# Five small moves in a TensorE-bound two-block transformer kernel: piece sizes, load order, and where adds, transposes and copies stand

## The reference

```python
for layer in range(2):
    x = x + 0.5 * swiglu(rms_norm(x, g[0]), ffn1_w_in[layer], ffn1_w_out[layer])
    h = rms_norm(x, g[1])
    x = x + (even_mixer(h, ...) if layer == 0 else odd_mixer(h, ...))
    x = x + memory_cross_attention(rms_norm(x, g[2]), rms_norm(mem, g[3]), ...)
    x = x + 0.5 * swiglu(rms_norm(x, g[4]), ffn2_w_in[layer], ffn2_w_out[layer])
# second block: three branches from one projection, gated and summed, then
x = x + mixed @ w_out
x = x + square(relu(rms_norm(x) @ w_ff1)) @ w_ff2
return rms_norm(x)
```

## Time and profile before

| | |
|---|---|
| median of 3 runs | 1675.61 us (1675.24 to 1676.27) |
| the profiled execution | 1676.27 us, its span 1674.8 us |
| PE busy | 1652.0 us, 99% |
| DVE, ACT, POOL busy | 66%, 52%, 14% |
| DMA | 293.05 MB, mean 175 GB/s |

### The profile page before, as it was taken

How to read it: one execution, slowest core, us unless ns; L and a number is a source line. 1 busy time by engine, 2 the same in 40 slices (tenths; PEclk the granted TensorE clock), 3 DMA queues, 4 the chain that set the end, 5 groups by cost and what they waited for, 6 DMA issues and landing times.

```text
span 1674.8 us, 21348 instructions
## 1 busy us (share of the span) xinstructions
PE 1652.0 (99%) x8136; PEld 1376.2 (82%) x8136; DVE 1102.3 (66%) x1744; ACT 864.4 (52%) x1323; POOL 236.4 (14%) x343
## 2 busy tenths in 40 slices
PE   7999999999999999999999999999999999999997
PEld 6888887788888888888889888888898778888886
DVE  5766788767656556555776685655568887775555
ACT  5555457665555445444544555544444446454444
POOL 2499701000000000000000000000044343100000
PEclk9999999999999999999999999999999999999999
DMA  8666755444455565655654453555574434555552
GB/s 250 203 214 202 228 158 186 144 140 138 146 195 179 187 187 177 189 188 189 201 163 141 162 162 123 183 187 189 188 237 141 134 120 136 187 191 189 189 180 97
DMA packets 185248, 293.05 MB, mean 175 GB/s; under 512 B 13527, under 2 KB 106234, under 8 KB 184250
## 3 DMA queue, kind: packets, MB, share of 16 engines
q1 hardware_dynamic: 180288, 274.81, 51.2%
q0 software_dynamic: 4368, 16.29, 3.1%
q10 hardware_dynamic: 490, 0.59, 0.1%
HBM read 286.12 MB, written 5.25 MB: 174 GB/s over the span
## 4 chain that ended last, share of the span: by engine, by line
PE 93%; DVE 4%; ACT 2%; issue 1%; ACTq 0%; DVEq 0%
PE b L432 28%; PE b L434 27%; PE b L433 27%; PE b L590 2%; PE b L553 1%; DVE wlo L1563 1%; PE b L566 1%; PE b L496 1%; PE b L939 1%; PE b L800 1%; PE b L951 1%; PE b L816 1%; PE b L538 1%; PE b L512 1%; ACT whi L1029 1%
## 5 line engine op out<-in xcount | busy, mean ns | idle before, releaser
L1563 DVE TENSOR_TENSOR wlo<-raw,whi 128x1024 fp32r<-128x1024 f32 (+1 forms) x523 | 653.3, 1252 | 465.3 <-ACT whi L1029 464.6
L1029 ACT ACTIVATE whi<-raw 128x1024 fp32r<-128x1024 f32 (+1 forms) x523 | 550.1, 1053 | 578.8 <-PE b L434 576.2
L432 PE MATMUL b<-whi,hT 128*128 128x512 f32 (+1 forms) x1184 | 468.9, 396 | 1.9 <-DVE wlo L1563 1.9
L434 PE MATMUL b<-whi,hT 128*128 128x512 f32 (+1 forms) x1184 | 459.0, 388 | 0.0
L433 PE MATMUL b<-wlo,hT 128*128 128x512 f32 (+1 forms) x1184 | 458.1, 387 | 0.0
L432 PEld LDWEIGHTS b<-whi,hT 128*128 128x128 f32 x1184 | 222.8, 188 | 53.1 <-issue 7.1
L432 PE MATMUL b<-whi,oT 128*128 128x512 f32 x672 | 264.8, 394 | 0.0
L434 PE MATMUL b<-whi,oT 128*128 128x512 f32 x672 | 261.9, 390 | 0.0
L433 PE MATMUL b<-wlo,oT 128*128 128x512 f32 x672 | 261.5, 389 | 0.0
L434 PEld LDWEIGHTS b<-whi,hT 128*128 128x128 f32 x1184 | 222.7, 188 | 46.7
L433 PEld LDWEIGHTS b<-wlo,hT 128*128 128x128 f32 x1184 | 223.1, 188 | 42.2 <-issue 0.5
(11 more groups left out here) (315 smaller groups left out, 1782.2 us busy)
## 6 DMA issues: line engine op xcount, KB each, us to landing
raw<-in_ffn_w_in SPq DMA_DIRECT2D x350, 256.0 KB, 3.0
raw<-in_ffn_w_out SPq DMA_DIRECT2D x88, 512.0 KB, 3.3
raw<-in_w_ff SPq DMA_DIRECT2D x64, 512.0 KB, 3.3
raw<-in_w_in SPq DMA_DIRECT2D x40, 512.0 KB, 3.6
raw<-in_x_w_kv SPq DMA_DIRECT2D x32, 512.0 KB, 3.5
raw<-in_even_w_in SPq DMA_DIRECT2D x24, 512.0 KB, 4.1
raw<-in_odd_w_in SPq DMA_DIRECT2D x24, 512.0 KB, 3.8
raw<-in_x_w_q SPq DMA_DIRECT2D x16, 512.0 KB, 3.9
```

The source lines that it names most:

```text
L432: T.matmul(out, ah, bh, start=start, stop=False, skip_group_check=skip)
L434: return T.matmul(out, al, bh, start=False, stop=stop, skip_group_check=skip)
L1029: E.activation(K.whi[j % NSPLIT][:, 0:n], K.raw[j % NRAW][:, 0:n], ACT.Copy).then_inc(*S.whi.done(j))
L1563: V.tensor_tensor(K.wlo[j % NSPLIT][:, 0:n], K.raw[j % NRAW][:, 0:n], K.whi[j % NSPLIT][:, 0:n].bitcast(F32), ALU.subtract).then_inc(*S.wl ...
```

## The change

Five moves, in words; all arithmetic and all matmuls stay.

1. `project_x` on DVE, in all five places: the split of piece 8 is issued ahead of the two adds, where it stood behind them.
2. Even mixer: the transposes of eB's third tile move on PE from behind piece 0 of kv01 to the end of av, ahead of `head_turn("ak")`; `diff_weigh(2)` moves from piece 1 to piece 0 of kv01; ACT's copy of the probabilities, its squares of the result and DVE's sum of these each move one piece forward.
3. `f0up0` is cut into eight pieces of one kt. With it the copies, squares and the norm factor of the first stage are put to other pieces.
4. POOL no longer waits for piece 20 before it loads `mem`.
5. SP issues the second part of the constants after piece 6.

```diff
-    G["f0up0"].cut([1, 1, 2, 2, 2])
+    G["f0up0"].per, G["f0up0"].n = 1, 8
@@ PE, even mixer
-                                         2: lambda: diff_weigh(1)})
+                                         2: lambda: diff_weigh(1), 3: lambda: prob_turn("eB", 2, 4)})
         head_turn("ak")
-        gemm("kv01", *headed("kv01"), None, {0: lambda: (prob_turn("eB", 2, 4), score_a(0)),
-                                             1: lambda: (diff_weigh(2), score_a(1)), 2: lambda: turn_a(0),
+        gemm("kv01", *headed("kv01"), None, {0: lambda: (diff_weigh(2), score_a(0)), 1: lambda: score_a(1), 2: lambda: turn_a(0),
@@ ACT, first stage
-                if c == 0 and p == 1:
+                if c == 0 and p == (1 if f.before else 2):
                     turned_halves(f.name, f.g0, K.hT, (2, 3))
-                if c == 0 and p == (1 if f.before else 3):
+                if c == 0 and p == (1 if f.before else 4):
                     x_squares(f.name, f.before, (1,))
@@ ACT, even mixer
             if p == 0:
+                probs("eB", 2)
                 head_copy("ak", K.kT, 0, [K.gain(121)])
                 copied("av", K.vsb[:, 0, :], K.vsb[:, 1, :])
             elif p == 1:
-                probs("eB", 2)
+                diff_square(1, 2)
                 item_exps("eA", 0)
             elif p == 2:
-                diff_square(1, 2)
                 query_sums(1)
@@ ACT, first stage
-    ffn(FFNS[0], {(0, 2): lambda: x_squares("f0", None, (0,)), (2, 1): step_sizes, (3, 0): angles}, {
+    ffn(FFNS[0], {(0, 1): lambda: x_squares("f0", None, (0,)), (2, 1): step_sizes, (3, 0): angles}, {
@@ DVE, project_x
+                    weights(K.at[f"{strips}{c}", order[2 * half + i]] + AHEAD)
+                    if at in beside:
+                        beside[at]()
                     if at == 6:
                         for t in range(2):
                             added(stage, t, 0, K.place[f"{strips}0"][t], 1.0, S.dense.at((f"{strips}0", t)))
-                    weights(K.at[f"{strips}{c}", order[2 * half + i]] + AHEAD)
-                    if at in beside:
-                        beside[at]()
@@ DVE, first stage
-                if c == 0 and p == 1:
+                if c == 0 and p == (1 if f.before else 2):
                     turned_lows(f.name, f.g0, K.hT, (2, 3))
-                if c == 0 and p == (2 if f.before else 4):
+                if c == 0 and p == (2 if f.before else 6):
                     row_rstd(f.name)
@@ DVE, even mixer
                 diff_sums(0)
+                diff_sums(1)
             elif p == 2:
                 item(1)
-                diff_sums(1)
                 diff_weighed()
@@ POOL
     small_loads()
-    pool.wait_ge(*S.loaded[0].at(20))
     mem_load(0)
@@ SP
-        elif j == 12:
+        elif j == 6:
             Q.dma_start(K.cst[:, P:CONST_N], D["consts"][:, P:CONST_N]).then_inc(*S.masks.done(0, step=16))
```

More of the change, by code:

```diff
@@ L268, in __init__ @@
         self.width = sum(w for _, w in cols)
[L269 to L275, removed]
+        self.per = SLOT // max(self.width, 256)
+        self.n = -(-KT // self.per)
 class Ffn:
@@ L438, in gemm_piece @@
         first, last = (n == 0 if first is None else first), (n == g.n - 1 if last is None else last)
-        k0, nk = g.begin[n], g.tiles[n]
+        k0, KT = n * g.per, g.KT
+        nk = min(g.per, KT - k0)
         hi, lo, j = piece(g.W[0], g.W[1], k0, nk, g.cols)
```

## The result

The changed kernel takes 1689.57 us in the median (1687.39 to 1690.01, four runs), the kernel before, measured beside it, 1675.94 (1675.24 to 1677.35). The ratio is 1.0078, 95% interval 1.006 to 1.0095. It is slower by about 13 us, where I had forecast 4.4 and had let the range end at 1683.6. (The ratios of this document are estimated from all runs and can differ from the quotient of the two medians by some ten-thousandths.) The direction was right, the size was not. The profiled execution took 1690.48 us; its span grew by 13.9 us.

A forecast was written before the change was run, and what follows sets the result against it. PE was taken as the bound, busy 1652.0 of 1674.8 us, so only its waits count. Projections +6.3, third tile -1.9 and start 0 gave +4.4 us, predicted 1680.3 us, range 1677.9 to 1683.6.

The forecast's parts named there:

- The queue behind the wait: Output projections: ACT's squares wait for the adds, ACT's split of piece 9 starts 1.46 us later, copies and lower halves follow.
- the row for the lower halves: Sign at the output projections: about 1 us of PE waits at line 432 for the lower halves of x.
- the wait at piece 8: Output projections: PE waits 0.2 us more at piece 8 for the lower halves, at each of five places.
- I take 0: Start of the kernel, moves 3 to 5: about nothing, with bounds from 0.2 us gained to 2.5 lost.
- rival 2: Start: `mem` and constants loads collide, piece 9 lands late, clock falls; 2.4 us over forecast, 1682.7 us; chance 0.12.
- Rival 1: Ahead of kv01: the clock falls all the same, move 2 gains 0.4 instead of 1.9 us, 1681.8 us; chance 0.26.

The follow-up runs named there:

- the start alone: Moves 3 to 5 without moves 1 and 2, against the kernel before: ratio 1.0023 (1.0014 to 1.0033), nine runs, +3.8 us.
- the constants behind piece 8: Move 3 with the constants issued after piece 8 and `mem` as late as before, against the kernel before: ratio 1.0013 (1.0003 to 1.0022), +2.1 us.
- the scaling first: Kernel before with one edit, DVE scaling the keys of eA ahead of `blend(2)`: 1674.41 against 1676.64 us, ratio 0.9993 (0.9984 to 1.0003).

## Why the prediction was wrong

**Move 1: right.** Forecast 1.05 + 0.2 = 1.25 for a place and 6.3 for five; measured 1.06 + 0.29 = 1.35 directly, 1.41 by the steps of move 1 alone, 6.9 to 7.5 in its time. The queue behind the wait (squares, split of piece 9, copies, lower halves) came out as written, only the row for the lower halves that I had named as a sign did not appear: ACT's copies start at 449.65 instead of 440.00; 8.0 of these 9.65 us had been lost before, so they are 1.6 late, where I had said 1.46. The term that was sized a little small is the wait at piece 8, 0.2 for 0.29.

**Moves 3 to 5: the step that failed is "I take 0".** This is the bulk of the miss: 3.8 us alone and 6.2 in the profiled execution, lower clock included, where rival 2, with 0.12, had 2.4. For piece 8 I had assumed that PE would hold ACT's split, as it did at 20.31, and a load held it, until 22.65. For piece 9 I had computed the danger (piece 9 landing at 24.5, ACT 0.3 us late) and then excused it with a reason that is false (it landed at 28.3): "fewer bytes are queued ahead of it now, since the early pieces are half as large". Smaller pieces do not put fewer bytes ahead of a needed byte. The buffers are counted in pieces, so they let the later weights be issued later, 13.5 us with the cut alone and 14.2 with the whole change instead of 10.5 for the first piece of `f0up1`. And the 452 KB of constants, which took 7.0 us to land, went in ahead of them. I had looked at the constants' move only as bytes, and not listed what stands behind them on SP's queue. Rival 2 named piece 9 and both loads; it was pieces 8 and 9, with two waits instead of one, and the constants by themselves give the loss in the times.

**Move 2: the size was right, the clock was not.** At the full clock the gain is 1.93, against 1.95 worked out. But the wait was 2.15 to 2.16 us, not 2.04, and of four profiled executions with it the clock fell in three. I argued from the nearest single row, 2.0 at line 590, that it would stay up. Rival 1 (0.26) is what happened in those three, and the whole move is worth 0.3 us then.

**The sum.** Terms measured alone: 7.5 (ratio of move 1) - 0.3 + 3.8 = 11.0, against 13.1 by the ratio of the whole. The rest, 2 us, lies within the intervals, and is of the size of one more loss of the clock: the profiled execution has one of 2.7 us behind two waits in the start, where the start alone had one behind a single wait. That the two belong together is argued, not shown.

## What to carry to other kernels

When a transfer moves forward in a queue, list what is now behind it and when that was last needed; a smaller piece size with a fixed number of buffers moves every later issue back by itself. What is put ahead of an add costs more than its own length where it has a wait of its own: the adds had 1.67 us to spare, but the split ahead of them also waits for ACT, so they came some 2.9 us later, and about 1.1 us of that was paid at each of the five places. And where PE is the bound, look first at what stands ahead of the instruction it waits for on the other engine; moving two DVE steps forward there gave 4.6 us, the clock that it kept included, more than any of these five moves gave or was worked out to give.

## What the runs showed of the hardware

The clock does not answer to the length of a wait alone. Behind waits of 1.5 us it stayed at 1.00 four times of four, behind those of 2.0 at line 590 nine times of eleven, behind those of 2.15 once of four, behind those of 2.75 twice of eight, and behind those of 3.7 it fell both times. The same instruction behind the same wait, with moves 4 and 5 alone (it was 1.00 in the earlier trace rows):

```profile
28.80:32.20 3.40, 3.35 (x10) 2.66 (x11) 2.97 (x4) 2.21 (x3) 0.00 (x0) 0.51 0.69 229
```

and behind the longer one, with the constants behind piece 8 (0.51 in the earlier trace rows):

```profile
300.12 1.23 PE L512 MATMUL b<-cst,sqj 128*128 128x128 f32 x8 [2.76 <-DVE sqj L1682]
```

```profile
300.10:303.50 3.40, 3.38 (x19) 2.81 (x20) 2.74 (x3) 2.90 (x5) 0.00 (x0) 1.00 0.41 139
```

At line 590 the falls go with the start: the two profiles that fell are those in which the clock had first come up at 15.2 and 15.3 us, and in the nine that kept it it had come up at 12.4 to 14.0. In front of kv01 no such order is seen (kept with 12.4, 13.0 and 13.7, lost with 12.8 to 15.2). What else decides there was not found.

Measured by the starts of the same matmuls, the clock that came up at 15.2 to 15.3 us instead of 12.8 cost 1.1 us, and the fall at line 590 cost 1.4, each in both profiles. Ahead of kv01 a fall is worth 1.6 us behind the wait of 2.15 (0.33 against 1.93 gained) and 1.4 behind that of 2.75 (what the profile with the constants behind piece 8 gains there on the one of before). The kernel before ran from 1674.8 to 1679.2 us in 75 executions. Its mean granted clock is on record for 71 of them: 11 with 0.998 took 1674.8 to 1675.8 us, 51 with 0.997 took 1675.6 to 1678.2, 9 with 0.996 took 1677.5 to 1679.2. So most of the spread of one kernel goes with the clock, and the three prices above, 3.9 us together, are of its size. The Trainium skill, "TensorE: Matmul & The Clock Gate", section "What's actually happening", says that the number of matmuls at the low clock differs between runs of one kernel; five profiles whose programs are the same up to 290 us (before, moves 1, 2, both, and the scaling first) agree, with a clock that came up at 12.8 to 15.3 us. One trace of a clock is a draw, and a term that hangs on it should be priced as a mean.
